# The activations act_t placed 128 bytes higher, f_t with its two buffers 320 bytes higher, the small tables packed around them

## The chip, the cores and the metric
The kernel runs on one core of a Trainium2 chip. The metric is the device time in microseconds (us) of one execution. Three executions of the kernel before took 1748.99, 1750.17 and 1750.59 us, a median of 1750.17 us.

## The reference
One decoder layer over 256 tokens of width 2048, in float32. The token mixer multiplies x by a wide input matrix, runs a sliding-window attention over 32 heads beside a gated linear recurrence over 2560 channels, projects both to 2048 columns, merges them by sigmoid gates and multiplies by an output matrix. A LayerNorm closes it. The channel mixer is a gated MLP of width 6144 with a three-tap convolution on the gate, and a second LayerNorm.

```python
proj = x @ w_in[l]
q, k, v, rx, ry, gl = jnp.split(proj, SPLIT_POINTS, axis=-1)
...
y_attn = sliding_window_attention(q, k, v, attn_sinks[l]) @ w_attn_proj[l]
rx = causal_dwconv(rx, rnn_conv_w[l], rnn_conv_b[l])
hr = rg_lru(rx, lru_wa[l], lru_ba[l], lru_wi[l], lru_bi[l], lru_lambda[l])
y_rnn = (hr * jax.nn.gelu(ry, approximate=True)) @ w_rnn_proj[l]
g_attn, g_rnn = jnp.split(jax.nn.sigmoid(gl + b_gate[l]), 2, axis=-1)
mix = (g_attn * y_attn + g_rnn * y_rnn) @ w_out[l]
x = layer_norm(ALPHA * x + mix, ln1_g[l], ln1_b[l])
up = x @ ffn_w_up[l]
gate = causal_dwconv(x @ ffn_w_gate[l], ffn_conv_w[l], ffn_conv_b[l])
f = (jax.nn.gelu(gate, approximate=True) * up) @ ffn_w_down[l]
x = layer_norm(ALPHA * x + f, ln2_g[l], ln2_b[l])
```

## The kernel before
Every weight matrix passes once through the core. SyncE's queue loads chunks of it into `raw`, ScalarE rounds half a chunk (a "unit") to the fp32r form `w_hi` (L239), VectorE writes the rest, `raw - w_hi`, to `w_lo` (L246), and TensorE multiplies. The activations are split in the same way, part 0 high and part 1 low, and each product is the sum of three passes: high by high, high by low, low by high. `w_hi` and `w_lo` have four slots each, so the two splitting engines run ahead of TensorE by some units.

There are two forms of product. In `panel_features` (L268) a 128x128 tile of the weights is stationary and 256 tokens of the activations are the moving operand, so a matmul streams 256 columns; the activations are `act_t` in the stages rxy, q, kv, gr, ga, ff0 and ff1, `g_t` in rnn, and `o_t` in attn. In `panel_tokens` (L295) the activations are stationary and 512 columns of the weights move; they are `act_t` in the stage out, and `f_t` in down0 and down1. The value half of the kv stage (L280) is of the second form with 256 columns. The stages follow each other as rxy (8 panels, with the recurrence's gates, L484, put between units), q, kv, rnn, gr, ga (attention's small matmuls between units), attn, out, ff0, down0, ff1, down1. A panel of `panel_features` with 512 columns of weights has 4 tiles x 16 x 3 passes = 192 matmuls.

All buffers are placed by hand at byte offsets in a partition, `BASE + offset`. The order of the work is written out by hand and hangs on semaphores.

Of the kernel before, what the change touches and what calls it, by code (L numbers as in the profile page):

```python
# [28 lines left out]
F32R = mybir.dt.float32r  # L29
# [4 lines left out]
P = 128  # L34
T = 256
TOK = T // P
D = 2048
KT = D // P
# [8 lines left out]
FT_HALF = D_FF // P // 2  # L47
# [51 lines left out]
def layer_kernel(nc, consts, x, w_in, b_gate, rnn_conv_w, rnn_conv_b, lru_wa, lru_ba, lru_wi, lru_bi,  # L99
# [4 lines left out]
    with ExitStack() as ctx:  # L104
        BASE = (nc.sbuf_base + 63) // 64 * 64

        def at(name, offset, shape, dt=F32):
            return nc.alloc_sbuf_tensor_at(name, shape, dt, offset=BASE + offset)
# [14 lines left out]
        v_now = raw_tail[:, 0, T:T + TOK * HD].rearrange("p (b d) -> p b d", b=TOK)  # L123
        probs_t = [raw_tail[:, 1, 0:3 * P], raw_tail[:, 2, 0:3 * P]]

        act_t = at("act_t", 81920 + 64, [P, KT, 2, T], F32R)
        SMALL = 81920 + 64 + 32768
        const = at("const", SMALL, [P, CONST_COLS])
        par = at("par", SMALL + 640, [P, PAR_COLS])
        sinks = at("sinks", SMALL + 2304, [P, NH])  # L130
        coef = at("coef", SMALL + 2432, [P, 9, RT])
        smax = at("smax", SMALL + 3168, [P, 4, 3])
        ssmall = at("ssmall", SMALL + 3232, [P, 5, 8])
        stats = at("stats", SMALL + 3392, [P, TOK, 4, 6])
        lnv = at("lnv", SMALL + 3584, [P, TOK, 6])
        ident = const[:, CONST_ID:CONST_ID + P]
        dist = raw_tail[:, 3, 0:3 * P]
        BIG = SMALL + 3648 + 64

        x_tok = at("x_tok", BIG, [P, TOK, D])  # L140
        par_rows = at("par_rows", BIG + 16384, [P, 4, P])

        g_t = at("g_t", BIG, [P, RT, 2, T], F32R)

        g_work = at("g_work", BIG, [P, RT, 2, T])
        xc = at("xc", BIG + 40960, [P, GRP, T])
        lru_r = at("lru_r", BIG + 46080, [P, GRP, T])
        lru_i = at("lru_i", BIG + 51200, [P, GRP, T])
# [17 lines left out]

        res = at("res", BIG, [P, TOK, D])
        ln_gb = at("ln_gb", BIG + 16384, [P, 2, D])
        f_t = at("f_t", BIG + 32768, [P, FT_HALF, 2, T], F32R)
        gate_c = at("gate_c", BIG + 81920, [P, 4, T])  # L170
        f_raw = at("f_raw", BIG + 86016, [P, 4, T])
        ln_t = at("ln_t", BIG + 32768, [P, KT, T])


# [1120 lines left out]
```

How the kernel before makes its waits and increments, by code:

```python
        def load_chunk(sp, w_rows, chunk, kc, width, col, rot, slot, first=False):  # L215
            if not first:
                sp.wait_ge(lo_made, rot * 8 + 2 * slot - 6)
            src = w_rows.rearrange("(k p) n -> p k n", p=P)[:, kc * chunk:kc * chunk + kc, ds(col, width)]
            sp.dma_start(raw[:, slot, 0:kc * width].rearrange("p (k n) -> p k n", k=kc), src)\
              .then_inc(raw_loaded[slot], 16)
# [7 lines left out]
        def split_hi(act, unit, j, size, refill=True):  # L230
            slot, chunk = j % 4, j // 2 % 4
            if j % 2 == 0:
                act.wait_ge(raw_loaded[chunk], (unit + j // 8 * 8) * 2 + 16)
            if refill:
                act.wait_ge(unit_used, unit + j - 3)
            half = j % 2 * size
            nc.scalar.activation(w_hi[:, slot, 0:size], raw[:, chunk, half:half + size], ACT.Copy)\
                .then_inc(hi_made, 1)
# [1 line left out]
        def split_lo(dve, unit, j, size):  # L242
            slot, chunk, half = j % 4, j // 2 % 4, j % 2 * size
            dve.wait_ge(hi_made, unit + j + 1)
            nc.vector.tensor_tensor(w_lo[:, slot, 0:size], raw[:, chunk, half:half + size],
                                    w_hi[:, slot, 0:size].bitcast(F32), ALU.subtract).then_inc(lo_made, 1)
# [3 lines left out]
        def panel_features(pe, unit, j0, acc, moving, kc, width, between=lambda j: None, columns=None):  # L251
# [4 lines left out]
            for j in range(8):  # L256
                slot = (j0 + j) % 4
                pe.wait_ge(lo_made, unit + j0 + j + 1)
                last = None
```

## Time and profile before
| | |
|---|---|
| median of three executions | 1750.17 us |
| the profiled execution | 1746.61 us |
| its span, first to last instruction | 1744.8 us |
| TensorE busy (matmul) | 1713.1 us, 98% of the span, 13020 matmuls |
| TensorE weight load busy | 1632.1 us |
| VectorE busy | 1026.4 us, 59% |
| ScalarE busy | 843.8 us, 48% |
| DMA | 317.15 MB, 182 GB/s |

A matmul's own duration in the profile contains its way through the array, during which the next has already begun. What a matmul costs in a dense stream is therefore the distance from its start to the next one's start, called pace here. It is read by dividing the length of a stretch by the matmuls in it, or from the start times of the timeline.

### The profile page before, as it was taken

How to read it: one execution, taken by the hardware profiler on the slowest of the kernel's cores; microseconds unless marked ns; L12 is line 12 of the kernel's file. 1: busy time of each engine (PE TensorE's matmuls, PEld its weight loads, DVE VectorE, ACT ScalarE, POOL GpSimd, SP SyncE). 2: the span in 40 equal slices, each digit the busy share in tenths (PEclk: the TensorE clock that was granted, in tenths of full speed). 3: DMA queues.
4: the chain of work that ended last, by engine and by line, in shares of the span. 5: the costliest groups of instructions: out<-in, count | busy, mean ns of one | idle time of the engine just before them, and what ended most of it. 6: DMA issues, size and time to landing. Idle time of an engine off the chain costs nothing.

```text
span 1744.8 us, 32111 instructions
## 1 busy us (share of the span) xinstructions
PE 1713.1 (98%) x13020; PEld 1632.1 (94%) x13020; DVE 1026.4 (59%) x1190; ACT 843.8 (48%) x1027; POOL 31.4 (2%) x30
## 2 busy tenths in 40 slices
PE   7999999999999999999999999999999999999996
PEld 7999999999999999999888999998889999999885
DVE  6696695444446666556557666655444556565556
ACT  5567566444346666644436444444333444444332
POOL 0000000000000000000000000000000000000002
PEclk9999999999999999999999999999999999999998
DMA  9364463565544344455754565565556555555551
GB/s 315 128 223 156 141 205 126 191 216 186 194 142 159 124 166 139 150 194 192 285 173 152 186 192 192 186 226 190 193 192 193 185 178 191 192 178 184 192 193 72
DMA packets 157142, 317.15 MB, mean 182 GB/s; under 512 B 6008, under 2 KB 11800, under 8 KB 156312
## 3 DMA queue, kind: packets, MB, share of 16 engines
q1 hardware_dynamic: 157080, 316.28, 54.5%
q8 instruction: 44, 0.72, 0.2%
q14 instruction: 18, 0.15, 0.0%
HBM read 314.16 MB, written 2.10 MB: 181 GB/s over the span
## 4 chain that ended last, share of the span: by engine, by line
PE 94%; DVE 2%; ACT 2%; issue 1%; DMA 0%; DVEq 0%; SPq 0%; ACTq 0%
PE bank L268 69%; PE bank L295 20%; PE bank L484 2%; PE bank L554 1%; PE bank L541 1%; PE bank L280 1%; ACT s_buf L787 1%; ACT w_hi L239 1%; PE bank L532 0%; ACT ln_t L845 0%; DVE s_buf L1028 0%; DMA x_tok<-in_x_dram 0%; DVE res L1239 0%; DVE res L1235 0%; DVE smax L1032 0%
## 5 line engine op out<-in xcount | busy, mean ns | idle before, releaser
L268 PE MATMUL bank<-act_t,w_hi 128*128 128x256 f32 x5952 | 1058.0, 280 | 8.2 <-DVE w_lo L246 8.2
L246 DVE TENSOR_TENSOR w_lo<-raw,w_hi 128x1024 fp32r<-128x1024 f32 (+1 forms) x552 | 694.7, 1271 | 610.4 <-ACT w_hi L239 610.2
L239 ACT ACTIVATE w_hi<-raw 128x1024 fp32r<-128x1024 f32 (+1 forms) x552 | 599.9, 1095 | 752.3 <-PE bank L268 547.2
L268 PEld LDWEIGHTS bank<-act_t,w_hi 128*128 128x128 f32 x5952 | 908.4, 188 | 12.6 <-issue 5.9
L268 PE MATMUL bank<-act_t,w_lo 128*128 128x256 f32 x2976 | 831.3, 279 | 0.0
L268 PEld LDWEIGHTS bank<-act_t,w_lo 128*128 128x128 f32 x2976 | 558.4, 188 | 0.0
L295 PE MATMUL bank<-w_hi,f_t 128*128 128x512 f32 x768 | 238.6, 392 | 0.0
L295 PEld LDWEIGHTS bank<-w_hi,f_t 128*128 128x128 f32 x768 | 144.2, 188 | 32.0
L295 PE MATMUL bank<-w_lo,f_t 128*128 128x512 f32 x384 | 150.2, 391 | 0.0
L268 PE MATMUL bank<-g_t,w_hi 128*128 128x256 f32 x640 | 113.1, 281 | 0.0
L268 PEld LDWEIGHTS bank<-g_t,w_hi 128*128 128x128 f32 x640 | 98.2, 190 | 0.0
L268 PE MATMUL bank<-g_t,w_lo 128*128 128x256 f32 x320 | 89.9, 281 | 0.0
L268 PE MATMUL bank<-o_t,w_hi 128*128 128x256 f32 x512 | 87.2, 276 | 0.0
L295 PEld LDWEIGHTS bank<-w_lo,f_t 128*128 128x128 f32 x384 | 72.1, 188 | 15.1
L295 PE MATMUL bank<-w_hi,act_t 128*128 128x512 f32 x256 | 80.6, 396 | 0.0
L268 PEld LDWEIGHTS bank<-o_t,w_hi 128*128 128x128 f32 x512 | 77.0, 188 | 0.2 <-issue 0.2
L268 PE MATMUL bank<-o_t,w_lo 128*128 128x256 f32 x256 | 70.7, 276 | 0.0
L268 PEld LDWEIGHTS bank<-g_t,w_lo 128*128 128x128 f32 x320 | 60.1, 188 | 0.0
L295 PEld LDWEIGHTS bank<-w_hi,act_t 128*128 128x128 f32 x256 | 48.1, 188 | 11.6
L295 PE MATMUL bank<-w_lo,act_t 128*128 128x512 f32 x128 | 50.6, 395 | 0.0
L268 PEld LDWEIGHTS bank<-o_t,w_lo 128*128 128x128 f32 x256 | 48.1, 188 | 0.0
L1186 DVE SCALAR_TENSOR_TENSOR gate_c<-bank,par,gate_c 128x255 f32<-128x255 f32 (+1 forms) x96 | 39.7, 475 | 3.6 <-DVE gate_c L1183 1.8
(137 smaller groups left out, 940.4 us busy)
## 6 DMA issues: line engine op xcount, KB each, us to landing
raw<-in_w_in_dram SPq DMA_DIRECT2D x52, 1024.0 KB, 5.0
raw<-in_ffn_w_gate_dram SPq DMA_DIRECT2D x48, 1024.0 KB, 5.1
raw<-in_ffn_w_up_dram SPq DMA_DIRECT2D x48, 1024.0 KB, 5.1
raw<-in_ffn_w_down_dram SPq DMA_DIRECT2D x48, 1024.0 KB, 5.1
raw<-in_w_in_dram SPq DMA_DIRECT2D x32, 1280.0 KB, 5.9
raw<-in_w_rnn_proj_dram SPq DMA_DIRECT2D x16, 1280.0 KB, 6.1
raw<-in_w_attn_proj_dram SPq DMA_DIRECT2D x16, 1024.0 KB, 5.1
raw<-in_w_out_dram SPq DMA_DIRECT2D x16, 1024.0 KB, 5.2
```

The costliest lines, as they stand in the source:

```text
L239: nc.scalar.activation(w_hi[:, slot, 0:size], raw[:, chunk, half:half + size], ACT.Copy)\
L246: nc.vector.tensor_tensor(w_lo[:, slot, 0:size], raw[:, chunk, half:half + size], w_hi[:, slot, 0:size].bitcast(F32), ALU.subtract).then_i ...
L268: last = nc.tensor.matmul(dst, w[:, slot, at_ % size:at_ % size + P], moving[:, kt, part, :], start=(kt == 0 and n == 0 and c % 2 == 0), s ...
L280: last = nc.tensor.matmul(acc[1][:, t * T:t * T + T], moving[:, kt, part, t * P:t * P + P], w[:, slot, at_ % size:at_ % size + width - col ...
L295: last = nc.tensor.matmul(acc[t][:, :], stationary[:, kt, part, t * P:t * P + P], w[:, slot, k * 512:k * 512 + 512], start=(kt == 0 and n ...
L484: done = nc.tensor.matmul(gate_bank[c][:, m * T:m * T + T], w[:, m, tile:tile + P], v[:, t, :], start=(t == feeds[0] and n == 0), stop=(t ...
L541: turned = nc.tensor.transpose(pt_bank[hh % 2][:, n * P:n * P + P], s_buf[:, hh, seg * P:seg * P + P], ident)
L554: nc.tensor.matmul(o_bank[pair][half:half + HD, 0:T], v_now[:, 0, :], probs_t[hh % 2][:, 0:T], start=True, stop=False, skip_group_check=True)
L787: nc.scalar.activation(s_buf[:, hh, c0:c1], s_buf[:, hh, c0:c1], ACT.Exp, scale=SCALE, bias=bias[:, 2 * hh + blk:2 * hh + blk + 1], accum_ ...
L1186: done = nc.vector.scalar_tensor_tensor(gate_c[:, c, k:T], src, tap, gate_c[:, c, k:T], ALU.mult, ALU.add)
```

## The change
Only allocations differ. `act_t` goes from offset 81984 to 82112, and the tables right behind it (`const`, `par`, `sinks`, `coef`, `ssmall`, `stats`) go up with it by 128 bytes. `smax` and `lnv` leave that block for the end of the memory, which closes the gap, so that `BIG` and with it `x_tok`, `g_t`, `o_t`, `res`, the recurrence's buffers and the attention's stay at the bytes they had. `f_t`, `gate_c` and `f_raw` go up by 320 bytes. Each engine has the same instructions in the same order.

```diff
-        act_t = at("act_t", 81920 + 64, [P, KT, 2, T], F32R)
-        SMALL = 81920 + 64 + 32768
+        act_t = at("act_t", 81920 + 192, [P, KT, 2, T], F32R)
+        SMALL = 81920 + 192 + 32768
...
-        smax = at("smax", SMALL + 3168, [P, 4, 3])
...
-        lnv = at("lnv", SMALL + 3584, [P, TOK, 6])
...
-        BIG = SMALL + 3648 + 64
+        BIG = SMALL + 3584
+        lnv = at("lnv", BIG + 94208, [P, TOK, 6])
+        smax = at("smax", BIG + 94208 + 64, [P, 4, 3])
...
-        f_t = at("f_t", BIG + 32768, [P, FT_HALF, 2, T], F32R)
-        gate_c = at("gate_c", BIG + 81920, [P, 4, T])
-        f_raw = at("f_raw", BIG + 86016, [P, 4, T])
+        f_t = at("f_t", BIG + 32768 + 320, [P, FT_HALF, 2, T], F32R)
+        gate_c = at("gate_c", BIG + 81920 + 320, [P, 4, T])
+        f_raw = at("f_raw", BIG + 86016 + 320, [P, 4, T])
```

The strides inside the operands are whole multiples of 512 bytes (a weight tile 512, a slot 5120, a part 1024, a k-tile 2048), so an operand's start modulo 256 is that of its buffer. From the offsets in the code, with the common `BASE` left out:

| buffer | offset mod 256 before | after |
|---|---|---|
| w_hi, w_lo | 0 | 0 |
| act_t | 64 | 192 |
| g_t, o_t | 192 | 192 |
| f_t | 192 | 0 |
| xc_hi, xc_lo, lru_w_hi, lru_w_lo | 192 | 192 |

## Rows read from the trace of the kernel before

**Rows 1.** The page: span, TensorE's busy time, its granted clock by slices, the chain.
```profile
span 1744.8 us, 32111 instructions
PE 1713.1 (98%) x13020; PEld 1632.1 (94%) x13020; DVE 1026.4 (59%) x1190; ACT 843.8 (48%) x1027; POOL 31.4 (2%) x30
...
PEclk9999999999999999999999999999999999999998
...
PE 94%; DVE 2%; ACT 2%; issue 1%; DMA 0%; DVEq 0%; SPq 0%; ACTq 0%
```

**Rows 2.** TensorE's longest waits: waiter, releaser, us in total, times, longest.
```profile
PE bank L268 <- DVE w_lo L246: 8.2, 4, 3.6
PE bank L456 <- DMA x_tok<-in_x_dram: 7.2, 2, 6.4
```

**Rows 3.** TensorE in stretches: from:to, length, busy us (xmatmuls), clock, DMA share, GB/s.
```profile
300.00:370.00 70.00, 70.00 (x597) 1.00 0.59 195
400.00:500.00 100.00, 100.00 (x851) 1.00 0.54 179
745.00:825.00 80.00, 80.00 (x708) 1.00 0.56 188
925.00:940.00 15.00, 15.00 (x134) 1.00 0.66 211
950.00:1190.00 240.00, 240.00 (x2040) 1.00 0.60 195
1200.00:1320.00 120.00, 120.00 (x526) 1.00 0.58 192
...
835.00:910.00 75.00, 75.00 (x323) 1.00 0.67 232
```

**Rows 4.** Timeline of TensorE at 710 us, attention's values, then act_t: start, length, instruction.
```profile
710.49 0.40 PE L556 MATMUL bank<-raw_tail 128*64 128x128 f32 x4
710.81 0.50 PE L268 MATMUL bank<-act_t,w_hi 128*128 128x256 f32 x2
711.15 0.28 PE L268 MATMUL bank<-act_t,w_lo 128*128 128x256 f32 x1
711.27 0.40 PE L268 MATMUL bank<-act_t,w_hi 128*128 128x256 f32 x2
711.51 0.28 PE L268 MATMUL bank<-act_t,w_lo 128*128 128x256 f32 x1
```

**Rows 5.** The same at 739 us, the same values, then o_t.
```profile
739.17 0.40 PE L556 MATMUL bank<-raw_tail 128*64 128x128 f32 x4
739.49 0.50 PE L268 MATMUL bank<-o_t,w_hi 128*128 128x256 f32 x2
739.83 0.28 PE L268 MATMUL bank<-o_t,w_lo 128*128 128x256 f32 x1
739.94 0.39 PE L268 MATMUL bank<-o_t,w_hi 128*128 128x256 f32 x2
740.17 0.28 PE L268 MATMUL bank<-o_t,w_lo 128*128 128x256 f32 x1
```

**Rows 6.** Timeline of TensorE at 395 us, the last of kv, then g_t.
```profile
395.32 0.28 PE L280 MATMUL bank<-w_hi,act_t 128*128 128x256 f32 x1
395.43 0.40 PE L268 MATMUL bank<-g_t,w_hi 128*128 128x256 f32 x2
395.67 0.28 PE L268 MATMUL bank<-g_t,w_lo 128*128 128x256 f32 x1
```

**Rows 7.** Timeline of TensorE at 941 us, from the first to the second panel of ff0.
```profile
941.08 0.51 PE L268 MATMUL bank<-act_t,w_hi 128*128 128x256 f32 x2 [0.56 <-DVE w_lo L246]
941.43 0.28 PE L268 MATMUL bank<-act_t,w_lo 128*128 128x256 f32 x1
```

**Rows 8.** Timeline of TensorE at 63 us, the recurrence's gates, first and last of twelve rows.
```profile
63.26 0.28 PE L484 MATMUL bank<-xc_hi,lru_w_hi 128*128 128x256 f32 x1
...
64.58 0.28 PE L484 MATMUL bank<-xc_hi,lru_w_lo 128*128 128x256 f32 x1
```

**Rows 9.** The page's groups: line, engine, operation, count | busy us, mean ns | idle before.
```profile
L268 PE MATMUL bank<-act_t,w_hi 128*128 128x256 f32 x5952 | 1058.0, 280 | 8.2 <-DVE w_lo L246 8.2
L246 DVE TENSOR_TENSOR w_lo<-raw,w_hi 128x1024 fp32r<-128x1024 f32 (+1 forms) x552 | 694.7, 1271 | 610.4 <-ACT w_hi L239 610.2
L268 PE MATMUL bank<-act_t,w_lo 128*128 128x256 f32 x2976 | 831.3, 279 | 0.0
L295 PE MATMUL bank<-w_hi,f_t 128*128 128x512 f32 x768 | 238.6, 392 | 0.0
```

## The prediction
> **What bounds the kernel now.** I read the page first. TensorE is busy for 1713.1 of 1744.8 us at its full granted clock, the 2.4 GHz level, and the chain of waits is 94% TensorE [rows 1]. The table of its waits comes next: the longest are 8.2 us on the split weights and 7.2 us on x at the start [rows 2]. VectorE, which splits the same weights, idles for 610 us, waiting for ScalarE and through it for TensorE's slots [rows 9]. So the kernel is a single stream of matmuls, and only the pace of that stream, or its number, can move the time. The number doesn't change here. An address can move the time only if it moves the pace.
>
> So the view to trust is the table of stretches, where all is dense [rows 3]. A stretch counts one or two matmuls that began before it; I take off two. The 256-column matmuls then have these paces: act_t in q 70/595 = 117.6 ns, act_t in ff0 240/2038 = 117.8 ns, g_t 100/849 = 117.8 ns, but o_t 80/706 = 113.3 ns, and act_t in the first panel of ff0 15/132 = 113.6 ns. The gates of the recurrence take 1.32 us for 11 steps, 120.0 ns [rows 8]. With 512 columns, out takes 75/321 = 233.6 ns and down 120/524 = 229.0 ns. These are the same engine, clock, shape, weight slots and number format, so there is a cost of 4 to 7 ns a matmul that isn't arithmetic. It is regular and lasts for hundreds of matmuls, which speaks against chance collisions with other engines or with DMA: the DMA share is 0.54 in the slow g_t stretch and 0.56 in the fast o_t one [rows 3].
>
> **What decides between 113.3 and 117.8.** Two things compete. One is the operands' place. The weights start at 0 modulo 256 (offsets as in the table of the change), act_t at 64, o_t at 192. The other is history: g_t has exactly o_t's place and still runs at 117.8, and act_t ran its first 192 matmuls of ff0 at 113.6 and all later ones at 117.8, in one place. Both paces are thus possible in both places, each holds itself, and a break or a change of operand can switch it. At 941 us a break of 0.56 us switched it from fast to slow [rows 7]. At 395 us the change from kv's last block to g_t switched it: steps of 0.11 us before, 0.24 us for two behind [rows 6].
>
> The clearest comparison for the change is the restart behind attention's values. The same small matmuls precede; then act_t starts, and its steps are 0.12, then 0.24 for two, 0.36 us for three [rows 4]. With o_t behind the same matmuls, the steps are 0.11, then 0.23 for two, 0.34 us for three, from the second row on [rows 5], and they stay so for 768 matmuls. The stages gr and ga put attention's small matmuls behind five of the eight units of each of their eight panels, 40 restarts. In the timeline the 39 that go on with act_t read like the one shown; the only one with o_t is fast. That is the evidence that place matters at a restart, and act_t now gets o_t's remainder, 192, against the same weights.
>
> **The change part by part.** (a) act_t as the moving operand. There are 5952 + 2976 = 8928 of these matmuls [rows 9]. 192 of them are fast already, and about half of the 96 in kv. The other 8690 or so go from 117.8 to 113.3 ns if all settle in o_t's pace: 8690 x 4.45 ns = 38.7 us, all of it on the path, since TensorE never stops. What could eat it is the supply. A unit of 24 matmuls would take 24 x 113.3 = 2.72 us against 1.27 us of VectorE for the same unit [rows 9], and the whole o_t stretch had this supply at this pace with busy time equal to its length [rows 3]. I therefore cost the loss of cover at nothing. The bounds of this term: above, the pace of the gates, where both operands start at the same remainder, 120.0 ns, gives +19 us; below, the fastest seen, 113.3, gives -38.7 us. No row shows less than 113.3 for a dense stream of 256 columns, and so nothing bounds a still better pace; I leave a small chance there. I take -38.7 us, as o_t's row is the one with the same pair of remainders.
>
> (b) act_t as the stationary operand in out, 384 matmuls of 512 columns (4 panels x 16 x 3 passes x 2). Before, the moving weights are at 0 and act_t at 64, 233.6 ns; f_t, at 192, has 229.0. act_t gets f_t's old remainder, so I take 384 x -4.5 = -1.7 us, with 0 and -2.6 (twice 113.3, 226.6 ns) as ends.
>
> (c) f_t as the stationary operand, 1152 matmuls (768 of them in the row, the rest with w_lo) [rows 9]. It goes to the remainder of the moving weights, 0. Only the gates have equal remainders, and they have 256 columns: twice 120.0 is 240.0 ns, +11 ns or +12.7 us. The other end is twice the fast pace, 226.6 ns, 1152 x -2.4 = -2.8 us. I take 0, its own row before, since the gates are short stretches between others and of another length.
>
> (d) g_t, 960 matmuls, doesn't move. It enters from kv, whose act_t has moved. If it is fast, -4.3 us; kv's last block was already fast before and g_t was slow behind it [rows 6], so 0.
>
> (e) All else that moves (gate_c, f_raw, the tables, smax, lnv) belongs to VectorE and ScalarE, whose work is hidden behind TensorE's; 0. If a softmax or LayerNorm instruction became slower by some per cent, the LayerNorms' waits of 8.2 us would grow by tenths [rows 2].
>
> The sum is -38.7 - 1.7 = -40.4 us. Against the profiled execution of 1746.61 us (span 1744.8) that is 1706.2 us; the executions' median is 3.6 us above the profiled one, so 1709.8 us there.
>
> The Trainium skill speaks against any of this. "SBUF — State Buffer", Who interferes with whom, gives TensorE two read ports, one for the moving operand and one for the weight load, and says it never waits on anyone; "TensorE: Matmul & The Clock Gate", Step-by-step, says that loading the next tile's weights doesn't steal read bandwidth from the running matmul. By that rule the place is nothing to TensorE, and the sum would be 0: the first rival below. This trace doesn't agree with a single cost per matmul: 113.3, 117.8 and 120.0 ns stand beside each other at 256 columns [rows 3, 8].
>
> **The rivals.** *The place is nothing, history is all* (the page's rule as a mechanism of this kernel). For it: g_t in o_t's place is slow for 960 matmuls, act_t in its own was fast for 192. Then the restarts fall as before, and the time is 1750 us, within 1. Against it: dozens of slow restarts of act_t against one fast of o_t in the same setting.
>
> *Partly.* The fast pace comes where a restart begins a stretch, but stretches entered without one keep the slow pace, as g_t's did. With gr and ga (8 panels, 1536 matmuls) and ff0 but not ff1, rxy and q: (1536 + 2112) x 4.45 = 16.2 us, 1734 us; with rxy and q too (1920 + 768), 12 us more, 1722 us.
>
> *Slower: f_t on the weights' own remainder.* If equal remainders cost what the gates show, down0 and down1 go from 229.0 towards 240.0 ns, and with act_t unchanged in its features the time is 1750.2 + 12.7 = 1763 us, less 1.7 us of out, 1761. For it: the gates are the slowest of the dense 256-column paces, and they alone have equal remainders. Against it: they run in blocks of 12 to 36 matmuls, and may pay for the changes of operand. It decides the sign if act_t gains less than 11 us, that is, if fewer than 2500 of its matmuls become fast.
>
> *Better than any row.* A pace below 113.3 ns, or fast f_t and g_t on top: 1698 us or less.
>
> **How the numbers follow.** The forecast, most of act_t at 113.3 ns (1700 to 1718 us), 0.38; partly (1718 to 1746) 0.22; no change 0.19; slower by f_t or by act_t at the gates' pace (up to 1769) 0.16; below 1700 0.05. A difference of over 0.2%, 3.5 us, is about what a measurement of this kernel can tell from none. So faster is 0.38 + 0.22 + 0.05 = 0.65, same 0.19, slower 0.16. The range 1698 to 1753 us leaves out most of the slower case and of the last, some 0.18.
>
> **What would show it.** Right: in the changed kernel's stretches 300 to 370 us and the middle of ff0, 113.3 ns a matmul (618 in 70 us in place of 597); restarts in gr and ga that settle in steps of 0.11; out at 229 ns. Step (c) shows in the middle of down0 as 524 matmuls in 120 us, or fewer. Wrong: 117.8 ns in all of act_t's stretches, or TensorE waiting for w_lo inside a panel, which would say that the supply bounds. The forecast stands or falls with one comparison, o_t against act_t behind the same matmuls; g_t is the row that speaks loudest against it.

## The result, and the profile after

| | before | changed |
|---|---|---|
| median | 1749.15 us (6 executions, 1744.85 to 1750.59) | 1730.59 us (6 executions, 1728.02 to 1737.93) |
| profiled execution, span | 1744.8 us | 1729.3 us |
| TensorE busy | 1713.1 us | 1696.2 us |

The ratio is 0.9903, with a 95% interval of 0.9883 to 0.9922. The change makes the kernel 1% faster, which is a clear gain, and less than half of the 40.4 us that were forecast.

The page of the changed kernel first:

```profile
span 1729.3 us, 32111 instructions
PE 1696.2 (98%) x13020; PEld 1618.0 (94%) x13020; DVE 1026.0 (59%) x1190; ACT 844.4 (49%) x1027; POOL 31.4 (2%) x30
```

Against [rows 1], only TensorE's busy times have moved, the matmuls' by 17 us; VectorE and ScalarE are as they were, and so is TensorE's clock (1.00 of full speed in every stretch below). So the pace of the matmuls is the right place to look. The stretches of the changed kernel have the columns of [rows 3] and answer to them: q, rnn, attn, ff0, down0, then ff1, which was not shown there, and out:

```profile
300.00:370.00 70.00, 70.00 (x597) 1.00 0.59 195
400.00:500.00 100.00, 100.00 (x885) 1.00 0.57 189
740.00:815.00 75.00, 75.00 (x639) 1.00 0.56 183
955.00:1175.00 220.00, 220.00 (x1944) 1.00 0.62 204
1190.00:1305.00 115.00, 115.00 (x509) 1.00 0.59 192
1320.00:1580.00 260.00, 260.00 (x2210) 1.00 0.57 186
825.00:900.00 75.00, 75.00 (x323) 1.00 0.68 240
```

The stretch of ff1 in the kernel before:

```profile
1330.00:1590.00 260.00, 260.00 (x2210) 1.00 0.57 184
```

Taking the matmuls at a stretch's ends off as before, q stays at 117.7 ns, g_t in rnn goes from 117.8 to 113.3, o_t in attn goes the other way, from 113.3 to 117.7, ff0 from 117.8 to 113.3, down0 from 229.0 to 226.8, out stays at 233.6, and ff1 stays at 117.8 (2208 matmuls in 260 us in both). With the boundaries of the stages taken from the timeline, the 15.5 us of the span come out as follows (the attention's matmuls and all waits are inside the stages):

| stage | before, us | changed, us | difference |
|---|---|---|---|
| start to rnn | 395.4 | 395.8 | +0.4 |
| rnn (g_t) | 113.1 | 108.8 | -4.3 |
| gr, ga (act_t) | 231.0 | 227.4 | -3.6 |
| attn (o_t) | 87.2 | 90.6 | +3.4 |
| out, LayerNorm and ff0 | 369.0 | 360.0 | -9.0 |
| down0 | 131.9 | 130.6 | -1.3 |
| ff1 | 271.3 | 271.3 | 0 |
| down1 and end | 146.0 | 144.8 | -1.2 |

Attn is the surprise, since neither o_t nor the weights have moved. The end of ga's last unit and attn's first matmuls in the changed kernel:

```profile
730.65 0.28 PE L268 MATMUL bank<-act_t,w_lo 128*128 128x256 f32 x1
...
730.99 0.28 PE L268 MATMUL bank<-act_t,w_lo 128*128 128x256 f32 x1
...
731.68 0.39 PE L556 MATMUL bank<-raw_tail 128*64 128x128 f32 x4
732.00 0.50 PE L268 MATMUL bank<-o_t,w_hi 128*128 128x256 f32 x2
732.34 0.28 PE L268 MATMUL bank<-o_t,w_lo 128*128 128x256 f32 x1
732.46 0.40 PE L268 MATMUL bank<-o_t,w_hi 128*128 128x256 f32 x2
732.69 0.28 PE L268 MATMUL bank<-o_t,w_lo 128*128 128x256 f32 x1
```

The end of ga's last unit in the kernel before:

```profile
738.12 0.28 PE L268 MATMUL bank<-act_t,w_lo 128*128 128x256 f32 x1
...
738.48 0.28 PE L268 MATMUL bank<-act_t,w_lo 128*128 128x256 f32 x1
```

The same operands, behind the same small matmuls, take 0.35 us for three steps (732.34 to 732.69) where [rows 5] have 0.34 (739.83 to 740.17), and they keep 117.8 ns to the end. What differs is the pace of the stream ahead of the small matmuls: three steps of ga's last unit took 0.36 us before (117.8 ns a matmul) and take 0.34 us now (113.3).

### The profile page after: what moved, and what is told of

Read it like the earlier page. It is cut to its first block, busy times and chain, and to the rows that moved or that the text cites. A ratio compares the mean times of both kernels' runs of the same rounds, so it can differ in the third digit from the quotient of the medians.

```text
span 1729.3 us, 32111 instructions
## 1 busy us (share of the span) xinstructions
PE 1696.2 (98%) x13020; PEld 1618.0 (94%) x13020; DVE 1026.0 (59%) x1190; ACT 844.4 (49%) x1027; POOL 31.4 (2%) x30
## 4 chain that ended last, share of the span: by engine, by line
PE 93%; DVE 3%; ACT 2%; issue 1%; DMA 1%; SPq 0%; DVEq 0%; ACTq 0%
PE bank L268 68%; PE bank L295 20%; PE bank L484 2%; ACT s_buf L787 1%; PE bank L554 1%; PE bank L541 1%; PE bank L280 1%; DMA raw<-in_w_in_dram 1%; DVE s_buf L1028 1%; DVE smax L1032 1%; PE bank L532 0%; DVE res L1239 0%; DVE res L1235 0%; ACT w_hi L239 0%; PE bank L556 0%
## 5 line engine op out<-in xcount | busy, mean ns | idle before, releaser
L268 PE MATMUL bank<-act_t,w_hi 128*128 128x256 f32 x5952 | 1044.1, 280 | 8.0 <-DVE w_lo L246 8.0
L268 PEld LDWEIGHTS bank<-act_t,w_lo 128*128 128x128 f32 x2976 | 564.4, 190 | 0.0
L268 PE MATMUL bank<-g_t,w_hi 128*128 128x256 f32 x640 | 108.9, 276 | 0.0
L268 PE MATMUL bank<-o_t,w_hi 128*128 128x256 f32 x512 | 90.6, 281 | 0.0
```

The costliest lines, as they stand in the source:

```text
L268: last = nc.tensor.matmul(dst, w[:, slot, at_ % size:at_ % size + P], moving[:, kt, part, :], start=(kt == 0 and n == 0 and c % 2 == 0), s ...
```

## The experiments

"Fast" and "slow" below mean 113.3 and 117.8 ns for 256 columns. The theory put to the test is this: the pace is a state of TensorE's stream that holds itself; a break or a change of operand can switch it; and the place of the operands, modulo 256, decides which paces there are and what a break does to them. The rivals are that place alone decides, and that history alone does. A pace given for a whole stage is the distance between two starts in it, divided by the matmuls between them.

**One move at a time.** The first kernel has only act_t and the tables moved; against the changed kernel its edit is the one below and the same for gate_c and f_raw. The second is the kernel before with those three lines as the changed kernel has them.

```diff
-        f_t = at("f_t", BIG + 32768 + 320, [P, FT_HALF, 2, T], F32R)
+        f_t = at("f_t", BIG + 32768, [P, FT_HALF, 2, T], F32R)
```

> The changed layout with f_t, gate_c and f_raw back at their old bytes, so only act_t and the tables have moved. If the two moves act apart from each other: down0 and down1 go back from 226.7 to 229.0 ns a matmul, 1152 x 2.3 = 2.6 us over the changed kernel, and gr, ga, rnn and ff0 stay at 113.3 ns, attn at 117.8; some 15 us under the kernel before. If f_t's place sets the pace that ff0 or ff1 keeps (a rival), ff1's pace changes too.

> The layout of before, with f_t, gate_c and f_raw alone 320 bytes up. Apart: down at 226.7 ns, everything else at the paces of before, 2.6 us under before. Rival: the whole gain of the features comes from history that begins in f_t's stages; then ff1 goes to 113.3 and the time is 13 us under before.

act_t alone gives 1721.45 us in the median of 9 (ratio 0.9868, 0.9838 to 0.9898), f_t alone 1742.2 us (0.9977, 0.9953 to 1.0002). f_t alone is as expected in the trace: down at 226.7 ns and all the long stretches at the paces of before. act_t alone isn't. It was expected some 3 us above the changed kernel and is 9 us below it in the medians. Its profiled execution was one of its two slowest, 1732.49 us, so it was profiled again.

> Only act_t and the tables moved, one more profile of it. Most of its executions took 1718 to 1722 us, but the one profiled before took 1732.5 us, with ff0 slow (117.8 ns), down0 at 233.3 and ff1 fast. If the 11 us between them are ff0's pace and what follows, a profile of a usual execution shows ff0 and ff1 both at 113.3 and both downs at 228.9. If f_t's place decides ff1 (f_t at remainder 192 hands a fast pace on, at 0 it turns it over), ff1 is fast behind a fast ff0 here, where the changed kernel has it slow. Rival: ff1 is always the opposite of ff0, and the 11 us lie elsewhere.

This execution took 1719.95 us. ff0, down0 and ff1 of the first and of the second profile of the same kernel:

```profile
955.00:1175.00 220.00, 220.00 (x1871) 1.00 0.60 196
1210.00:1305.00 95.00, 95.00 (x409) 1.00 0.57 188
1340.00:1570.00 230.00, 230.00 (x2032) 1.00 0.60 194
```

```profile
955.00:1175.00 220.00, 220.00 (x1944) 1.00 0.62 204
1210.00:1305.00 95.00, 95.00 (x417) 1.00 0.58 190
1340.00:1570.00 230.00, 230.00 (x2031) 1.00 0.59 192
```

ff0 was slow in the first (117.7 ns) and fast in the second (113.3), and down0 233.4 and 228.9 ns; ff1 was fast in both. So the first expectation of the two holds, and ff1 isn't the opposite of ff0. The same instructions at the same bytes give two paces in two executions: place alone doesn't decide. And behind a fast ff0, ff1 is fast with f_t at remainder 192 and slow with f_t at 0; later profiles of other kernels here with the same places agree. That is 10.3 us lost (2304 x 4.45 ns) for the 2.6 us that f_t's move gains in down, 7.7 us net. The two kernels lie 9 us apart by their medians and 6 us by their ratios, which were taken against different runs of the kernel before; the intervals of the ratios overlap (0.9883 to 0.9922 and 0.9838 to 0.9898), so the profiles show the loss in ff1, and the times only point the same way.

**The changed kernel again.**

> The changed kernel as it is, profiled once more. If the pace behind a break is a matter of chance with act_t at remainder 192, some stretch differs from the first profile: q behind its break of 1.86 us (slow there, fast with act_t alone) or ff0 behind the one of 0.8 us. gr, ga, rnn, down0, down1 read the same, and ff1 is the opposite of ff0. If place alone decides, all stretches read the same.

1727.11 us. The first lines are the changed kernel's q behind its break in the first profile, the second ones those of this one (timeline: start, length, instruction), and the third its stretch from 300 us:

```profile
294.23 0.50 PE L268 MATMUL bank<-act_t,w_hi 128*128 128x256 f32 x2 [1.58 <-DVE w_lo L246]
294.57 0.28 PE L268 MATMUL bank<-act_t,w_lo 128*128 128x256 f32 x1
294.68 0.40 PE L268 MATMUL bank<-act_t,w_hi 128*128 128x256 f32 x2
294.92 0.28 PE L268 MATMUL bank<-act_t,w_lo 128*128 128x256 f32 x1
```

```profile
293.88 0.50 PE L268 MATMUL bank<-act_t,w_hi 128*128 128x256 f32 x2 [1.58 <-DVE w_lo L246]
294.22 0.28 PE L268 MATMUL bank<-act_t,w_lo 128*128 128x256 f32 x1
294.33 0.39 PE L268 MATMUL bank<-act_t,w_hi 128*128 128x256 f32 x2
294.56 0.28 PE L268 MATMUL bank<-act_t,w_lo 128*128 128x256 f32 x1
```

```profile
300.00:370.00 70.00, 70.00 (x620) 1.00 0.61 200
```

The same wait of 1.58 us, and a different pace behind it for the rest of q, 684 matmuls: 597 of them in 70 us in the one, 620 in the other. All the long stretches from rnn on read alike in both, ff1 slow behind a fast ff0. A share of the scatter between executions, here 1727 to 1731 us, is thus a draw made at a break.

**g_t and o_t in all profiles.** g_t and o_t lie at one place against the same weights in every kernel of this document, so the paces at which they begin compare history at equal place. In all 16 profiles it goes one way. g_t begins at 117.8 ns where the last block of kv ahead of it ran at 113.3 to 113.6 (5 profiles), and at 113.3 where that block ran at 117.8 to 120.3 (11). o_t begins at 117.8 where the last unit of ga ran at 113.3 (8 profiles), and at 113.3 where it ran at 116.7 to 120.0 (8). So here the passage turns a fast stream slow and any slower one fast. It explains g_t's gain and attn's loss in the changed kernel: kv's last block turned slow (three steps of 0.36 us up to 395.60 us), ga's last unit fast.

**Extra matmuls as a switch.** If the pace is a state, something small should be able to switch it. Seven single matmuls of the other form were put in, into a part of PSUM that nobody reads, with act_t stationary and a loaded weight slot moving:

```diff
+        def extra(slot, out):
+            nc.tensor.matmul(out, act_t[:, 0, 0, 0:P], w_hi[:, slot, 0:T], start=False, stop=False, skip_group_check=True)
...
                 pe.wait_ge(lo_made, unit + j0 + j + 1)
+                if flip and j == flip[0]:
+                    extra(slot, flip[1])
...
-                panel_features(pe, i * 16, 8, ACC[1], act_t, 4, 640, between=between)
+                panel_features(pe, i * 16, 8, ACC[1], act_t, 4, 640, between=between, flip=(7, bank[5][:, T:2 * T]))
```

The calls of q, attn and ff1 get such an argument in the same way, for their first panel alone; for that the loops over the panels of q and attn and the first turn of ff1's are written out.

> The changed kernel with 7 extra matmuls of 256 columns, act_t stationary and a weight slot moving, into parts of PSUM that nobody reads: one in the last unit of each of the recurrence's four passes, one in q, one at the start of attn and one at the start of ff1. Theory of history (a pace is a state of the stream that a passage through the other operand form flips, and the steady stream keeps): each turns 117.8 into 113.3 ns behind it: about 1300 matmuls of rxy, 680 of q, 767 of attn, 2300 of ff1, together 5000 x 4.45 = 22 us less than the changed kernel, if g_t's 960, whose pace depends on the kv blocks ahead, stay fast; 18 us if they turn slow. Theory of place: the operands' bytes are as they were, so nothing changes, or 1 us more for the extra matmuls.

> The same 7 extra matmuls on the kernel before, with the old bytes. Theory of history: behind them rxy, q, ff1 go to 113.3 (about 4300 matmuls, 19 us under before), attn goes from 113.3 to 117.8 (3.4 us back), ff0, which has no extra matmul, stays slow behind its break; some 16 us under before. Theory of place: act_t at remainder 64 can't hold 113.3 for long except by accident, and nothing changes.

On the changed kernel's layout: 1716.77 us in the median of only 4 (0.9833, 0.9781 to 0.9885), with executions from 1708 to 1729. That is 14 us under the changed kernel by the medians, where 18 or 22 us were expected, and the intervals touch. The profiled execution is the slowest of the four, and its ff0 turned slow at a wait of 0.54 us in the first panel, which has no extra matmul. ff1 around its extra matmul (L253), with the products now on L274, and its stretch from 1340 us:

```profile
1322.91 0.28 PE L274 MATMUL bank<-act_t,w_lo 128*128 128x256 f32 x1
1323.03 0.40 PE L274 MATMUL bank<-act_t,w_hi 128*128 128x256 f32 x2
1323.26 0.28 PE L274 MATMUL bank<-act_t,w_lo 128*128 128x256 f32 x1
1323.38 0.28 PE L253 MATMUL bank<-w_hi,act_t 128*128 128x256 f32 x1
...
1324.08 0.28 PE L274 MATMUL bank<-act_t,w_lo 128*128 128x256 f32 x1
1324.19 0.39 PE L274 MATMUL bank<-act_t,w_hi 128*128 128x256 f32 x2
1324.42 0.28 PE L274 MATMUL bank<-act_t,w_lo 128*128 128x256 f32 x1
```

```profile
1340.00:1570.00 230.00, 230.00 (x2031) 1.00 0.59 192
```

Three steps take 0.35 us ahead of it (1322.91 to 1323.26) and 0.34 us behind (1324.08 to 1324.42), and the remaining 2280 matmuls of ff1 run at 113.3 ns. In attn the one extra matmul did the same for 744 matmuls, and out, with nothing changed in it, went from 233.3 to 228.9 ns behind the fast stream. In rxy each of the four switched the 150 matmuls behind it, up to a short wait for the weights, after which some stretches were fast and some slow. In q the break had already given the fast pace, and the extra matmul turned it back to slow, with g_t slow behind it: it flips, it doesn't mend. History, then, is real, and it alone moved ff1.

On the layout of before, the same seven matmuls did nothing: 1748.53 us (1.0017, 0.9992 to 1.0042). The stretch of its ff1 behind the extra matmul:

```profile
1340.00:1570.00 230.00, 230.00 (x1955) 1.00 0.58 187
```

ff1, rxy and q stayed slow, and attn stayed fast. I had expected 16 us from history. So with act_t at remainder 64 the slow pace survives what switches it at 192. Neither rival holds alone: there is a state, and the place decides how it is passed on. Whose place it is, that of the stream or that of the extra matmul's own act_t, this pair doesn't tell; attn, whose stream has the same bytes in both, was switched in the one and kept its pace in the other.

**The gates moved.** The gates' weights (lru_w, lru_w_lo, lru_w_hi) go 64 bytes up and xc_lo 256, on the changed kernel:

```diff
-        lru_w_hi = at("lru_w_hi", BIG + 74752, [P, 2, LRU_TILES * P], F32R)
+        lru_w_hi = at("lru_w_hi", BIG + 74752 + 64, [P, 2, LRU_TILES * P], F32R)
...
-        xc_lo = at("xc_lo", BIG + 88064, [P, GRP, T], F32R)
+        xc_lo = at("xc_lo", BIG + 88064 + 256, [P, GRP, T], F32R)
```

> The changed kernel with the gates' weights 64 bytes up (remainder 0) and xc_lo 256 bytes up (192 as before), so that the gates' two operands no longer start at equal remainders but 64 apart, moving 192 against stationary 0, as o_t or act_t against w_hi. If equal remainders are the gates' cost, they go from 120.0 to 113.3 or 117.8 ns, 312 x 2 to 6.7 = 0.7 to 2.1 us. If it is the passage through them that sets rxy slow each time, rxy's 1500 and q's 757 go to 113.3, 10 us more. Rival, the gates are slow because their blocks are short: nothing changes.

1732.91 us (0.9913, 0.9887 to 0.994), no different from the changed kernel. In the profile the gates went from 120.0 to 117.8 ns (the timeline has 1.76 us for 15 steps from 65.77 to 67.53 us), so the equal remainders were their cost and not their shortness. rxy stayed slow (300 matmuls in the 35 us from 85 us, 117.4 ns). That doesn't clear the equal remainders, though: in this execution the stream was already slow ahead of the first gates, where the two profiles of the changed kernel have it at 113.3 ns.

```profile
35.00:65.00 30.00, 30.00 (x257) 1.00 0.60 205
```

The last two kernels below answer it, since they differ in the gates' places alone.

**Other places of act_t.** One profile and one execution each, with 0, 128, 160, 96 and 32 in place of 192. In the first two f_t moves too (by 64 and 192 bytes); in the last three it has its old bytes.

```diff
-        act_t = at("act_t", 81920 + 192, [P, KT, 2, T], F32R)
+        act_t = at("act_t", 81920 + 0, [P, KT, 2, T], F32R)
```

> act_t at offset 81920, remainder 0 modulo 256 like the weights; f_t 64 bytes above its place before, remainder 0 too, but 256 modulo 512 where the changed kernel has 0. If equal remainders cost what the gates show, all of act_t's features run at 120.0 ns: 8928 x 2.2 = 20 us over the kernel before, some 1768 us. If only the remainder modulo 256 counts for f_t, down stays at 226.7 ns; if 512 counts, it is anything else.

> act_t at offset 82048, remainder 128, f_t 192 bytes above its place before, remainder 128: half a period from the weights' 0. If the distance modulo 128 decides (equal halves collide), it reads like remainder 0: 120.0 ns in the features. If it is the distance modulo 256, 128 is the farthest and may be faster than any row so far, below 113.3. Down: 226.7 in the first case.

> Only act_t and the tables moved, f_t at its old bytes, act_t at offset 82080, remainder 160: 96 from the weights' 0 modulo 256. If the cost goes by 64-byte blocks (160 lies in the block of 128), features read like remainder 128, 118.7 to 120.0 ns and about 1758 us. If it goes smoothly with the distance, between those and 113.3. If 96 lies outside of any collision, a pace that needs no luck: 113.3 or less in all stretches, rxy and q too, 1705 us or less.

> The same with act_t at offset 82016, remainder 96. By 64-byte blocks it reads like remainder 64 (the kernel before): 117.8 ns everywhere, 1746 us. If the distance to the weights counts smoothly or by its size alone (96 either way round), it reads like remainder 160.

> The same with act_t at offset 81952, remainder 32. By 64-byte blocks it reads like remainder 0: 120.0 ns flat and 1758 us. Otherwise between 113.3 and 120.0.

The stretches of ff0 and ff1 with act_t at remainder 0, then 32, 96, 128 and 160, each of its own kernel:

```profile
955.00:1175.00 220.00, 220.00 (x1836) 1.00 0.57 183
1340.00:1570.00 230.00, 230.00 (x1919) 1.00 0.57 182
```

```profile
955.00:1175.00 220.00, 220.00 (x1888) 1.00 0.59 196
1340.00:1570.00 230.00, 230.00 (x1974) 1.00 0.57 187
```

```profile
955.00:1175.00 220.00, 220.00 (x1835) 1.00 0.56 183
1340.00:1570.00 230.00, 230.00 (x1919) 1.00 0.56 182
```

```profile
955.00:1175.00 220.00, 220.00 (x1856) 1.00 0.58 190
1340.00:1570.00 230.00, 230.00 (x1919) 1.00 0.57 183
```

```profile
955.00:1175.00 220.00, 220.00 (x1877) 1.00 0.58 192
1340.00:1570.00 230.00, 230.00 (x1941) 1.00 0.57 184
```

| remainder of act_t (weights at 0) | ff0, ff1, ns a matmul | one execution, us |
|---|---|---|
| 0 | 120.0, 120.0 | 1757.75 |
| 32 | 116.7, 116.7 | 1735.41 |
| 64 (the profile of before) | 117.8, 117.8 | 1746.61 |
| 96 | 120.0, 120.0 | 1763.21 |
| 128 | 118.7, 120.0 | 1758.21 |
| 160 | 117.3, 118.7 | 1751.82 |
| 192 (act_t alone, second profile; the first had 117.8, 113.3 and 1732.49) | 113.3, 113.3 | 1719.95 |

At remainder 0 all of act_t's 256-column stages are flat at 120.0 ns, rxy and q too, as the gates' row had foretold. Blocks of 64 bytes don't describe it: 32 differs from 0 and 96 from 64. Remainder 32 has one pace in all of act_t's long stretches of its one profile, 116.7 ns. For the stationary side, f_t at remainder 0 gave 226.7 ns in down at 256 modulo 512 as it does at 0, and act_t at remainder 0 gave 226.7 ns in out; f_t at 128 gave 232.4 and 233.3. With 512 columns moving, equal remainders are the best place seen; with 256 columns they are among the worst. In these five kernels the tables stay where the changed kernel has them, so act_t's place does this and not theirs. That 256 bytes are the period is tested for f_t alone: all places of act_t lie within one stretch of 256.

**A version that takes the best of these.** act_t alone moved, f_t at its old bytes, and five extra matmuls, in rxy (four) and in attn; the second kernel has the gates moved as well, as above. Against act_t alone, beside `extra` and the call in rxy:

```diff
-                    panel_features(pe, i * 16 + UNITS["attn"], 8 * pp, acc_of("attn", pp), o_t, 4, 512,
+                    panel_features(pe, i * 16 + UNITS["attn"], 8 * pp, acc_of("attn", pp), o_t, 4, 512,
+                                   flip=(1, bank[6][:, 0:T]) if i == 0 and pp == 0 else None,
```

> Only act_t and the tables moved, f_t at its old bytes, and five extra matmuls: one in the last unit of each of the recurrence's four passes and one in attn's second unit; none in q or ff1. By the state and map theory: against 1720 us of act_t alone, rxy gains 4 x 150 x 4.45 = 2.7 us, attn 744 x 4.45 = 3.3 us, out 1.7 us, so some 1712 us. If the extra matmuls did not cause the switches seen with them, 1720 us.

> The same with the gates' weights 64 and xc_lo 256 bytes up: the gates at 117.8 in place of 120.0 ns, 312 x 2.2 = 0.7 us less again, if the extra matmul behind them still switches rxy; if it switches only behind equal remainders, 2 us more.

1718.21 us (0.9828, 0.9802 to 0.9855) and 1717.74 us (0.9829, 0.9808 to 0.9849). Both are some 0.75% faster than the changed kernel, clear of its interval (0.9883 to 0.9922), but can't be told from act_t alone (0.9838 to 0.9898) or from each other; 1712 us were expected. In attn the switch worked (fast, out at 228.9 ns), and in the first kernel in rxy too, but the draw ahead of the long stages is larger than what they bring: the profiled execution of the first took 1740 us, with ff0 and ff1 slow, and is left out of its ratio; the fastest of its executions took 1711.6 us.

The pair, one profile of each, also answers what the gates do to the pace of rxy. From 65 to 80 us the gates' matmuls and units of act_t take turns. The first line is of the first kernel, with the gates' operands at equal remainders, the second of the second, with them 64 bytes apart:

```profile
65.00:80.00 15.00, 15.00 (x128) 1.00 0.41 147
65.00:80.00 15.00, 15.00 (x135) 1.00 0.43 155
```

Both enter the first gates at 113.3 ns. In the first kernel the gates run at 120.0 ns and the units behind them at 117.8, in each of the four passes. In the second the gates too run at 113.3 ns and hand the fast pace on, in the first and the third pass; in the second and the fourth the stream comes in slow, and gates and units stay at 117.8 up to the extra matmul. In every profile here in which a fast stream met gates at equal remainders, it left them slow. So it is the equal remainders that turn a fast rxy slow at the gates. And since the stream arrived fast in the first and the third pass of the second kernel, the extra matmul there turned it slow (393 matmuls in the 46 us from 82 us): it flips in rxy too.

## Why the prediction was wrong

The bound was right. Only the pace moved, no long wait took its place, and the supply kept up at 113.3 ns. The longest waits in the changed kernel are the same but for one: the small matmuls of attention wait 2.2 us for VectorE where they waited 0.8 before, which fits TensorE being there earlier. The lines are two of the changed kernel and, apart, the last one's row in the kernel before:

```profile
PE bank L268 <- DVE w_lo L246: 8.0, 3, 4.0
...
PE bank L541 <- DVE s_buf L1056: 2.2, 3, 1.2
```

```profile
PE bank L541 <- DVE s_buf L1056: 0.8, 1, 0.8
```

The step that failed is (a), "if all settle in o_t's pace". The size of one switch, 4.45 ns, was right; the number of matmuls wasn't. Of the 8690 some 3750 became fast in the first profile: the start of rxy up to the first gates (360), most of gr and ga (1240) and ff0 (2150 beyond those that were fast before). The rest of rxy, q and ff1 stayed slow. 3750 x 4.45 is 16.7 us in place of 38.7. In the stage table the stages that hold them became only 12.2 us shorter: 2.0 us went at the start, where the first matmul came later and the first 120 took 15.2 us in place of 14.1, 1.9 us around attention's small matmuls (1.4 of it the longer wait), and 0.6 us in ff0 and ahead of it. So "all of it on the path" was not quite right either. The case called "partly", with gr, ga and ff0, had 16.2 us and 1734 us, and described what happened to act_t; I gave it 0.22 and the full one 0.38. That its time comes within 4 us of the measured one is in part luck: g_t's gain and attn's loss, which it doesn't have, cancel to 0.9 us, and f_t's gain stands against the waits.

The reason behind it was a comparison that showed less than I took it for. o_t fast against act_t slow, behind the same small matmuls and both behind a stream at 117.8 ns, does show an effect of the place; but it shows what that place makes of a slow stream, and I read it as the pace in which the place settles. With act_t at that very place, the restart behind attention's values gave the slow pace, for act_t (the first unit of each panel of gr and ga, 117.8 ns) and for o_t itself, since the stream ahead was now fast. The row that I called the loudest against me, g_t slow in o_t's place, was the one to believe: it began behind a fast block of kv. One reading was wrong beside this: the break at 941 us [rows 7] lies inside ff0's first panel, behind 144 matmuls, and not between two panels behind 192; the sum hardly moves by it.

(b) Out was forecast 1.7 us faster and didn't move, 233.3 ns. The runs show that the pace ahead of it matters too: it goes to 228.9 behind a fast attn (the extra matmul) with act_t at 192.

(c) f_t was taken at 0, between ends of -2.8 and +12.7 us. It came at the lower end, 226.7 ns in place of 228.9, -2.6 us. The gates' row at equal remainders said nothing on 512 columns, though it told truly what 256 would do. What f_t's move costs elsewhere, ff1, was in none of the terms.

(d) g_t was taken at 0 and gave 4.3 us, because kv's last block, which I took to stay fast, turned slow. (e) Nothing came of the rest, as forecast: VectorE and ScalarE are as busy as before. The 8.2 us that I called the LayerNorms' waits are not theirs alone; 3.6 us lie at the start of rxy and 1.6 us in q. Attn's 3.4 us of loss had no term at all, since its operands don't move.

The Trainium skill's rule ("SBUF — State Buffer", Who interferes with whom) is that TensorE's two read ports are independent and that it never waits on anyone. As a rule that the operands' places are nothing to each other, which is how the prediction used it, these runs don't agree with it: moving act_t by 64 to 192 bytes against the weights changed a 256-column matmul from 113.3 to 120.0 ns, with no other engine's work changed. Whether the ports are where that arises, no run here shows.

What stays open is the mechanism inside TensorE that holds the state, why a break in q or in ff0 leaves the pace one way or the other while the passages to g_t and o_t never differed, and what ff1 takes over from a slow ff0 (fast in the first profile of act_t alone, slow in that of the version with five extra matmuls, f_t at the same bytes). No run here looks inside it.

## What to carry to other kernels

In a kernel bound by TensorE, read the pace as start to start, stage by stage, before anything else; where two stages of one shape differ by some per cent, the operands' start modulo 256 is a cheap thing to try, the moving and the stationary form each for itself. A pace that two executions of one kernel disagree on is a state, so a layout is judged by several executions and more than one profile. Compare places only at equal history: a stage can change without one of its bytes having moved, and one comparison at one history tells what a place makes of that history, not where it settles.

## What the hardware showed that I had not expected

A single extra matmul of the other form switched the pace of the 2280 that followed, 117.8 to 113.3 ns, 10 us for 0.1 us; at another place of act_t it did nothing. The passages to g_t and o_t turned the pace over each time, from fast to slow and from anything slower to fast, 32 in 16 profiles. Gates with both operands at equal remainders turned a fast stream slow, and the same gates 64 bytes apart let it through. The paces are few and sharp: 113.3, 117.8 and 120.0 ns with 256 columns, 226.7, 228.9 and 233.3 with 512 at the multiples of 64 bytes other than 128; at 32, 116.7 ns stood beside them. The kernel before may have the draw as well: its executions in the experiments' comparisons ran from 1734 to 1751 us, though it has only one profile.
